# Second attention of a two-layer decoder: score products shared by a pair's two heads, on 128 rows

## The reference, cut to what matters

```python
def _swa_sink_attention(h, w_q, g_q, k_band, v_band, sinks, rel_bias, w_out):
    q = _rmsnorm((h @ w_q).reshape(bsz, seq, SWA_Q_HEADS, HEAD_DIM), g_q)
    s = einsum('bnqkgd,bnjkd->bnkgqj', qb, k_band) * (HEAD_DIM ** -0.5)
    s = s + bias            # a T5 bucket of the distance, per head
    s = where(0 <= dist < WINDOW, s, -inf)
    p = softmax(concatenate([s, sink], axis=-1), axis=-1)[..., :-1]
    o = einsum('bnkgqj,bnjkd->bnqkgd', p, v_band)
    return o.reshape(bsz, seq, -1) @ w_out
```

## Time and profile before

| what | value |
|---|---|
| median of 3 runs | 1274.31 us (1271.7 to 1276.66) |
| span of the profiled execution, first to last instruction | 1267.8 us (the page lists no other time of it) |
| mean granted TensorE clock | 0.984 of full speed |
| PE busy | 1226.4 us (97%), 5794 products |
| PEld busy | 1010.5 us (80%) |
| DVE / ACT / POOL busy | 576.1 / 478.2 / 558.5 us |
| chain that ended last | PE 68%, issue 15%, DVE 7%, POOL 6%, ACT 3% |
| second attention, first pass of pair 0 to end of pair 7 | 697.1 to 870.3 us |

### The profile page before, as it was taken

How to read it: one execution, slowest core, us unless ns; L and a number is a source line. 1 busy time by engine, 2 the same in 40 slices (tenths; PEclk the granted TensorE clock), 3 DMA queues, 4 the chain that set the end, 5 groups by cost and what they waited for, 6 DMA issues and landing times.

```text
span 1267.8 us, 15311 instructions
## 1 busy us (share of the span) xinstructions
PE 1226.4 (97%) x5794; PEld 1010.5 (80%) x5794; DVE 576.1 (45%) x717; ACT 478.2 (38%) x594; POOL 558.5 (44%) x383
## 2 busy tenths in 40 slices
PE   6999999999999999999999799999999999999998
PEld 6877877777888888888887678777788888888887
DVE  5857778867533001333116676866743200133100
ACT  4248778753322112222227244443332211222221
POOL 4513423415655444565445320221655544566532
PEclk9999999999999999999999699989999999999999
DMA  6221211112333353333333101110333333323341
GB/s 219 80 66 34 55 45 33 59 41 69 99 99 99 100 166 99 94 92 83 97 99 100 34 1 33 34 34 1 100 100 99 100 100 99 91 89 92 103 116 42
DMA packets 142238, 101.24 MB, mean 80 GB/s; under 512 B 3128, under 2 KB 141552, under 8 KB 142192
## 3 DMA queue, kind: packets, MB, share of 16 engines
q1 hardware_dynamic: 142128, 100.56, 26.8%
q10 hardware_dynamic: 64, 0.03, 0.0%
HBM read 98.47 MB, written 2.12 MB: 79 GB/s over the span
## 4 chain that ended last, share of the span: by engine, by line
PE 68%; issue 15%; DVE 7%; POOL 6%; ACT 3%; DMA 0%; SPq 0%; POOLq 0%; ACTq 0%; DVEq 0%
PE ps L1210 21%; PE ps L1212 21%; PE ps L1211 21%; POOL w_lo L410 5%; POOL fox_sq_lo L417 1%; PE ps L1556 1%; PE ps L1555 1%; DVE xn_lo L854 1%; DVE rst L826 1%; DVE x_hat L847 1%; DVE swa_diag L1157 1%; PE ps L1570 1%; ACT w_hi L469 1%; DMA x_in<-in_x 0%; PE ps L1557 0%
## 5 line engine op out<-in xcount | busy, mean ns | idle before, releaser
L410 POOL TENSOR_TENSOR w_lo<-stage,w_hi 128x512 fp32r<-128x512 f32 x356 | 519.9, 1490 | 487.8 <-ACT w_hi L469 480.2
L469 ACT ACTIVATE w_hi<-stage 128x2048 fp32r<-128x2048 f32 x88 | 168.4, 1914 | 475.2 <-PE ps L1212 470.4
L1210 PE MATMUL ps<-xn_hi,w_hi 128*128 128x512 f32 x720 | 285.3, 396 | 0.3 <-issue 0.3
L1212 PE MATMUL ps<-xn_hi,w_lo 128*128 128x512 f32 x720 | 281.0, 390 | 0.0
L1211 PE MATMUL ps<-xn_lo,w_hi 128*128 128x512 f32 x720 | 280.9, 390 | 0.0
L1210 PE MATMUL ps<-r_hi,w_hi 128*128 128x512 f32 x512 | 199.8, 390 | 0.0
L1212 PE MATMUL ps<-r_hi,w_lo 128*128 128x512 f32 x512 | 199.3, 389 | 0.0
L1211 PE MATMUL ps<-r_lo,w_hi 128*128 128x512 f32 x512 | 199.2, 389 | 0.0
L1210 PEld LDWEIGHTS ps<-xn_hi,w_hi 128*128 128x128 f32 x720 | 135.5, 188 | 30.6 <-issue 2.7
L1211 PEld LDWEIGHTS ps<-xn_lo,w_hi 128*128 128x128 f32 x720 | 135.5, 188 | 29.2 <-issue 1.9
L1212 PEld LDWEIGHTS ps<-xn_hi,w_lo 128*128 128x128 f32 x720 | 135.4, 188 | 28.6
(11 more groups left out here) (208 smaller groups left out, 1716.9 us busy)
## 6 DMA issues: line engine op xcount, KB each, us to landing
stage<-in_w_up SPq DMA_DIRECT2D x32, 1024.0 KB, 5.5
stage<-in_w_down SPq DMA_DIRECT2D x32, 1024.0 KB, 5.7
stage<-in_w_in_a SPq DMA_DIRECT2D x16, 512.0 KB, 5.0
stage<-in_w_in_a SPq DMA_DIRECT2D x4, 1024.0 KB, 6.2
stage<-in_w_out_a SPq DMA_DIRECT2D x4, 1024.0 KB, 5.2
stage<-in_w_q_b SPq DMA_DIRECT2D x4, 1024.0 KB, 5.1
stage<-in_w_out_b SPq DMA_DIRECT2D x4, 1024.0 KB, 5.2
x_in<-in_x SPq DMA_DIRECT2D x4, 512.0 KB, 7.3
```

The costliest lines, as they stand in the source:

```text
L410: ins = nc.gpsimd.tensor_tensor(w_lo[:, s, c], stage[:, s, c], w_hi[:, s, c].bitcast(F32), ALU.subtract)
L469: nc.scalar.activation(w_hi[:, s, :], stage[:, s, :], ACT.Copy).then_inc(w_hi_ready, 1)
L1210: mm(out_, st_hi, mv_hi, start=start, stop=False)
L1212: return mm(out_, st_lo, mv_hi, start=False, stop=stop)
```

## The change

Scores. The two heads of a pair share a product: key block kb of both heads goes to bank 2 + kb as 2 x 256 columns (2 x 128 for the last), so 40 products of up to 256 columns become 20 of up to 512. The key's low half is multiplied with all 128 rows, as are the products of the first pass. For this the first pass now waits for the low halves (`swa_lo_ready`), and for the sinks of the pair before having been read; the scores wait for the diagonals of both heads.

Exponentials. ScalarE takes bank after bank, both heads in one instruction, as each of the four finishes. The sink rows go to banks 2 and 3 once these are read, so they wait for exponentials, not for the stored output any more; the first output product waits for that. The output products go by query block, both heads in each.

```diff
 def swa_hi(i):
     act.wait_ge(swa_normed, i + 2)
+    after(act, swa_scores_done, TB * i)
     for e in range(2):
-        after(act, swa_scores_done, 2 * i - 1 + e)
         ins = nc.scalar.activation(q_hl[own, e, :], qkn[own, 0, :], ACT.Copy)
-def swa_exp(j, e):
-    act.wait_ge(swa_scores_done, 2 * j + e + 1)
-    after(act, swa_out_done, 2 * j - 1 + e)
-    b = 2 + 2 * e
-    nc.scalar.activation(swa_p[:, e, 0:512], ps[:, b, :], ACT.Exp)
-    nc.scalar.activation(swa_p[:, e, 512:896], ps[:, b + 1, 0:384], ACT.Exp)
-    nc.scalar.activation(psink[e][:], ps[:, 6 + e, :], ACT.Exp, bias=...).then_inc(swa_probs_ready, 1)
+def swa_exp(j, kb):
+    act.wait_ge(swa_scores_done, TB * j + kb + 1)
+    after(act, swa_out_done, 2 * j)
+    n = 2 * P if kb < TB - 1 else P
+    nc.scalar.activation(swa_p[:, :, 2 * P * kb:2 * P * kb + n],
+                         ps[:, 2 + kb, 0:2 * n].rearrange("p (e n) -> p e n", e=2), ACT.Exp
+                         ).then_inc(swa_probs_ready, 1)
+def swa_sink(j, e):
+    act.wait_ge(swa_sinks_done, 2 * j + e + 1)
+    after(act, swa_den_ready, 2 * j)
+    nc.scalar.activation(psink[e][:], ps[:, 2 + e, :], ACT.Exp, bias=...).then_inc(swa_sinks_ready, 1)
+def swa_probs(j):      # called in place of the two swa_exp
+    for kb in range(TB):
+        swa_exp(j, kb)
+    for e in range(2):
+        swa_sink(j, e)
...
 def swa_lo(i):         # VectorE
-    after(dve, swa_scores_done, 2 * i)
+    after(dve, swa_scores_done, TB * i)
 def swa_max(j):        # before the diagonal is written
-        after(dve, swa_scores_done, 2 * j - 1 + e)
+        after(dve, swa_sinks_done, 2 * j - 1 + e)
 def swa_den(j):
         dve.wait_ge(swa_out_done, 2 * j + e + 1)
+        dve.wait_ge(swa_sinks_ready, 2 * j + e + 1)
...
 def swa_max_scores(j): # TensorE
-    pe.wait_ge(swa_hi_ready, j + 2)
+    pe.wait_ge(swa_lo_ready, j + 2)
+    after(pe, swa_sinks_ready, 2 * j)
-            mm(ps[:, bank, c0:c0 + n], q_hl[h, e, qb * P:(qb + 1) * P], kd_hi[h, g, k0:k0 + n],
+            mm(ps[:, bank, c0:c0 + n], q_hl[:, e, qb * P:(qb + 1) * P], kd_hi[:, g, k0:k0 + n],
                start=start, stop=False)
 def swa_scores(j):
-    pe.wait_ge(swa_lo_ready, j + 2)
-    for e in range(2):
-        pe.wait_ge(swa_diag_ready, 2 * j + e + 1)
-        for kb, bank, c0 in ((0, b, 0), (1, b, 256), (2, b + 1, 0), (3, b + 1, 256)):
-            o = ps[:, bank, c0:c0 + n]
-            mm(o, kd_hi[:, g, ks], q_hl[:, e, qs], start=True, stop=False)
-            mm(o, kd_lo[h, g, ks], q_hl[h, e, qs], start=False, stop=False)
-            mm(o, ones_r[:], swa_diag[:, e, qs], start=False, stop=False)
-            mm(o, anti_r[:], hk_lo[:, 2 * j + e, 0:n], start=False, stop=False)
-            mm(o, anti_r[:], hk_hi[:, 2 * j + e, 0:n], start=False, stop=True)
-        after(pe, swa_out_stored, 2 * j - 1 + e)
-        mm(ps[:, 6 + e, :], ones_r[:], swa_diag[:, e, :], ...).then_inc(swa_scores_done, 1)
+    pe.wait_ge(swa_diag_ready, 2 * j + 2)
+    for kb in range(TB):
+        n = 2 * P if kb < TB - 1 else P
+        o = ps[:, 2 + kb, 0:2 * n].rearrange("p (e n) -> p e n", e=2)
+        mm(o, kd_hi[:, g, ks], q_hl[:, :, qs], start=True, stop=False)
+        mm(o, kd_lo[:, g, ks], q_hl[:, :, qs], start=False, stop=False)
+        mm(o, ones_r[:], swa_diag[:, :, qs], start=False, stop=False)
+        mm(o, anti_r[:], hk_lo[:, 2 * j:2 * j + 2, 0:n], start=False, stop=False)
+        mm(o, anti_r[:], hk_hi[:, 2 * j:2 * j + 2, 0:n], start=False, stop=True).then_inc(swa_scores_done, 1)
+    for e in range(2):
+        pe.wait_ge(swa_probs_ready, TB * j + e + 1)
+        mm(ps[:, 2 + e, :], ones_r[:], swa_diag[:, e, :], ...).then_inc(swa_sinks_done, 1)
 def swa_pv(j):
-    for e in range(2):
-        pe.wait_ge(swa_probs_ready, 2 * j + e + 1)
-        for qb in range(TB):
+    after(pe, swa_out_stored, 2 * j)
+    for qb in range(TB):
+        pe.wait_ge(swa_probs_ready, TB * j + qb + 1)
+        for e in range(2):
             for kb in range(max(qb - 1, 0), qb + 1):
                 ins = mm(ps[:, 6 + e, ...], swa_vx[...], swa_p[:, e, src:src + P], ...)
```

More of the change, by code:

```diff
@@ L282, in build @@
         swa_scores_done = sem("swa_scores_done")
+        swa_sinks_done = sem("swa_sinks_done")
+        swa_sinks_ready = sem("swa_sinks_ready")
         swa_probs_ready = sem("swa_probs_ready")
@@ L727, in swa_hi @@
                 act.wait_ge(swa_normed, i + 2)
+                after(act, swa_scores_done, TB * i)
                 for e in range(2):
                     own = slice(64 * e, 64 * e + 64)
-                    after(act, swa_scores_done, 2 * i - 1 + e)
                     ins = nc.scalar.activation(q_hl[own, e, :], qkn[own, 0, :], ACT.Copy)
                 ins.then_inc(swa_hi_ready, 1)
-            def swa_exp(j, e):
-                act.wait_ge(swa_scores_done, 2 * j + e + 1)
-                after(act, swa_out_done, 2 * j - 1 + e)
-                b = 2 + 2 * e
-                nc.scalar.activation(swa_p[:, e, 0:512], ps[:, b, :], ACT.Exp)
-                nc.scalar.activation(swa_p[:, e, 512:896], ps[:, b + 1, 0:384], ACT.Exp)
-                nc.scalar.activation(psink[e][:], ps[:, 6 + e, :], ACT.Exp, bias=sinkb[:, 2 * j + e:2 * j + e + 1]
-                                     ).then_inc(swa_probs_ready, 1)
+            def swa_exp(j, kb):
[4 more added lines that the diff above has]
+                                     ps[:, 2 + kb, 0:2 * n].rearrange("p (e n) -> p e n", e=2), ACT.Exp
+                                     ).then_inc(swa_probs_ready, 1)
+            def swa_sink(j, e):
+                act.wait_ge(swa_sinks_done, 2 * j + e + 1)
+                after(act, swa_den_ready, 2 * j)
+                nc.scalar.activation(psink[e][:], ps[:, 2 + e, :], ACT.Exp, bias=sinkb[:, 2 * j + e:2 * j + e + 1]
+                                     ).then_inc(swa_sinks_ready, 1)
+            def swa_probs(j):
[3 more added lines that the diff above has]
+                    swa_sink(j, e)
             def swa_rec(j):
@@ L774, in _ @@
                         out_hi(1, swa_out_stored, c)
-                swa_exp(j, 0)
-                swa_exp(j, 1)
+                swa_probs(j)
                 swa_hi(j + 1)
@@ L784, in _ @@
                 out_hi(1, swa_out_stored, c)
-            swa_exp(7, 0)
-            swa_exp(7, 1)
+            swa_probs(7)
             out_hi(1, swa_out_stored, 6)
@@ new lines, in swa_scores @@
+                pe.wait_ge(swa_diag_ready, 2 * j + 2)
+                for kb in range(TB):
+                    n = 2 * P if kb < TB - 1 else P
+                    ks, qs = slice(kb * P, (kb + 1) * P), slice(kb * P, kb * P + n)
+                    o = ps[:, 2 + kb, 0:2 * n].rearrange("p (e n) -> p e n", e=2)
[4 more added lines that the diff above has]
+                    mm(o, anti_r[:], hk_hi[:, 2 * j:2 * j + 2, 0:n], start=False, stop=True).then_inc(swa_scores_done, 1)
@@ L1563, in swa_pv @@
+                for e in range(2):
+                    pe.wait_ge(swa_probs_ready, TB * j + e + 1)
+                    mm(ps[:, 2 + e, :], ones_r[:], swa_diag[:, e, :], start=True, stop=True).then_inc(swa_sinks_done, 1)
             def swa_pv(j):
                 g = j // (PAIRS // 2)
-                for e in range(2):
-                    pe.wait_ge(swa_probs_ready, 2 * j + e + 1)
-                    for qb in range(TB):
+                after(pe, swa_out_stored, 2 * j)
+                for qb in range(TB):
+                    pe.wait_ge(swa_probs_ready, TB * j + qb + 1)
+                    for e in range(2):
@@ L1571, in swa_pv @@
                                      swa_p[:, e, src:src + P], start=(kb == max(qb - 1, 0)), stop=(kb == qb))
-                    ins.then_inc(swa_out_done, 1)
+                        if qb == TB - 1:
+                            ins.then_inc(swa_out_done, 1)
             swa_proj(0, True, (0, 2))
@@ L1604, in _ @@
             swa_pv(PAIRS - 1)
+            pe.wait_ge(swa_sinks_ready, 2 * PAIRS)
             out_piece(1, 0, both, range(4, 7))
```

6 lines of the change are left out of this document (removed).

## The result

| | before | after |
|---|---|---|
| median | 1275.47 us (4 runs, 1271.7 to 1276.66) | 1236.11 us (4 runs, 1234.05 to 1237.48) |
| profiled execution: span | 1267.8 us | 1234.4 us |
| mean granted TensorE clock | 0.984 | 0.993 |
| TensorE busy, products | 1226.4 us, 5794 | 1186.5 us, 5634 |

The ratio is 0.9698, 95% interval 0.9676 to 0.972: 39 us faster by the medians, 33.4 by the spans of the two profiled executions. The forecast was 1241, with a range of 1233 to 1252; it started from the median of three of these four runs of before, 1274.31.

The account below looks back on a forecast made before the run. TensorE's own work was taken to bound the second attention. Pair gains of 5.9 + 11.8 + 6.1 + 7.1 + 2.9 = 33.8 us, less 0.8, took the span from 1267.8 to 1234.8; with 6.5 on top, 1241 us, range 1233 to 1252.

Parts of the forecast that it names:

- Scores from 7.4 to 4.0 us: Score products per pair on TensorE: 3.4 us less, 2.6 from the row switch and some 0.8 from joining heads.
- The formula that the prediction took: Warm product spacing N/2.4 + 2.5 ns: 109 ns for 256 columns, 216 for 512, so joining alone gains nothing.
- First pass 1.8 us: First products of each pair, now on 128 rows: some 0.9 us per head, 0.65 us less per pair.
- clean pairs: Pairs 1, 3 and 5, without a weight split: 16.0 us each, gaining 3.9 each, 11.8 in all.
- Output products 3.57 us: Each pair's output products on TensorE: same number in another order, still 3.57 us.
- The chain S+8.33: From scores' start S through exponentials, sinks, high halves and low halves: next first pass starts 8.33 us later.
- Split pairs 17.5: Pairs 2 and 4, where GpSimd's weight split slows VectorE: 17.5 us each, gaining 3.0 each, 6.1 in all.
- Pair 0: Scores released at 712.15 by both diagonals, 1.7 us for a half-clock stretch, end at 722.2: 5.9 us gained.
- Half clock behind the new waits: Rival: four half-clock stretches of some 2 us behind new waits; gain 25, time 1249; chance 0.14.
- The prediction's case against: Against half clock behind new waits: 1.75 us of TensorE idle from 886.9 left the clock at 1.00.
- The distance of 6.5 us: Median of the runs, 1274.31, over the profiled span, 1267.8; assumed to stay as it is after the change.
- the 0.8 taken off for pair 6: Allowance of 0.8 us for one more half-clock stretch behind pair 6's wait, cutting the gain to 33.

Follow-up runs that it names:

- rows only: Kernel before, with only the product of the keys' low half (L1555) put on all 128 rows; 1244.82 us, ratio 0.977.
- exponentials late: Changed kernel, with a pair's first exponential waiting for all four key blocks instead of its own bank; 1245.45 us, ratio 0.9777.
- high halves first: Changed kernel, with ScalarE making the next pair's high halves before the two sink exponentials; 1231.13 us, ratio 0.9687.
- split later: Changed kernel, with ScalarE's weight split in pairs 2, 4 and 6 moved behind the next query's reciprocal-root steps; 1232.9 us, ratio 0.9686.

## Why the prediction was right, and where it was off

- *Scores from 7.4 to 4.0 us, most of it the row switch.* Right: 729.97 to 733.96 is 3.99. By the runs, rows alone are 27 us of the 36 to 39, and the joining 3 to 4 in the finished form; the rest is the moved sink products and the exponentials block by block, which no run takes apart. The rule of the Trainium skill ("TensorEngine Tiling (Array Packing)", Key Properties) that a change of tiling mode drains the engine agrees with the block that went from 0.98 to 0.59 us when only the rows changed; no record shows the drain itself. The formula that the prediction took from the Trainium skill ("TensorE: Matmul & The Clock Gate", Back-to-back issue gap) agrees less well than the prediction says: 109 and 216 ns against 0.12 and 0.227 us, and the joining, which gains nothing by it, did gain.
- *First pass 1.8 us.* It took 1.97 (722.08 to 724.05), so 0.5 less and not 0.65: 1.04 for the first head, whose four products cost 0.52, and 0.93 for the second, where they cost 0.41; some 0.9 for each was forecast. Together with 0.02 in the projection and 0.02 in the chain this is why clean pairs took 16.25 us and not 16.0, 0.7 us less gained in the three of them.
- *Output products 3.57 us.* They took 3.29: the 0.27 us in which they waited for the second head's sink exponential before had been in that figure. It made the wait at the pair's end 0.6 in place of 0.3, and pair 7 13.44 in place of 13.7. The pair's length was set by the chain and did not move.
- *The chain S+8.33.* Right to 0.02; exponentials late shows that it sets the clean pairs, high halves first that 0.87 us of it is above TensorE's own work.
- *Split pairs 17.5.* Right; split later shows that VectorE's slow instructions are the cause.
- *Pair 0.* Forecast to end at 722.2, measured 722.08, with TensorE 0.3 us earlier at its start: 5.7 us gained, not 5.9. The scores were released at 712.02 by the second diagonal, and one stretch of 3.4 us at half clock followed. It came in this execution and not in the second one, so this term was a guess that fell right.
- *Half clock behind the new waits.* It did not come in the changed kernel's first profile in pairs 1 to 7; in the second it came once, behind the 2.35 us wait in pair 6, and cost 0.3 us. Whether it comes varies: 1.57 us waits left the clock whole each time, 1.83 in rows only brought it down, and so did 0.38 in one execution of before. The prediction's case against, 1.75 us of idle from 886.9, is sound, though its row shows the clock within the idle time only: it was 1.00 behind it too.
- *The distance of 6.5 us.* This was the term mis-sized. Time less span measured 1.8; the other 4 to 5 us lay in runs of before that were slower than its profiled execution. In the runs with both on record the longer spans have the lower clock (1268.4 us at 0.984, 1274.1 at 0.977), so half-clock time is the likely cause; for the three runs behind 1274.31 it is not shown. Taking spans alone, 1234.8 was forecast and 1234.4 came. That closeness is in part luck: clean pairs gained 0.7 us less and pair 0 0.2 less, while pair 7 gained 0.3 more, TensorE reached pair 0 0.3 us earlier, and the 0.8 taken off for pair 6 was not needed. By the medians the gain is 36 to 39 us and not 33. An extra half-clock stretch lasted 10.2 us in before and cost its pair 2 4.1 us; in the changed kernel one lasted 3.4 us and cost pair 6 0.3. That this makes the difference is an inference, since no run holds the clock fixed.

## What to carry to other kernels

A product on fewer rows between products on all rows costs its neighbours too: price it by the distances of starts around it, not by its own record. When the busiest engine is relieved, follow the chain behind its last product to the next one by hand; here it set the pair 0.9 us (clean) to 2.2 us (split) above TensorE's own 15.4, and two moves on other engines took that back. And compare spans with spans: one profiled execution can be 5 us quicker than the median of the same program.

## What the runs showed of the hardware that was not expected

The granted clock fell behind a wait of 0.38 us in one execution and not behind 1.57 in another; in two executions of the same kernel it fell behind a 2.35 us wait in pair 6 and stayed whole behind 2.36. And it came back sooner with the products on 128 rows: in pair 0 it stayed half for 20.5 us in both profiles of the kernel before, with TensorE busy from 710.2 on, and for 6.8 in rows only, where the scores' 64-row products alone had changed. The runs show both, not the rule behind them.

One GpSimd instruction of 4.6 us held a VectorE instruction of 0.69 us for 4.3 us; moved and cut into four of 1.4, it cost 0.5 us in pair 1 and pair 0 won 5.2, of which 1.7 is a half-clock stretch that did not come.
